# Width-grouped k steps in the two-segment stages, and modulation units summed on all partitions, in a two-layer hybrid trunk

## The reference, cut to what matters

```python
mod_x = jnp.einsum('bd,lde->lbe', jax.nn.silu(c), w_ada) + b_ada[:, None, :]
mod_c = jnp.einsum('d,lde->le', jax.nn.silu(c_ctx), w_ada) + b_ada
for i in range(DEPTH):
    sh1, sc1, g1, sh2, sc2, g2 = jnp.split(mod_x[i][:, None, :], 6, axis=-1)   # and csh1 ... cg2
    hx = rmsnorm(x, norm_mix[i]) * (1.0 + sc1) + sh1                           # hc likewise
    ox, oc = gla_mixer(...) if i % N_MIXERS == 0 else swa_mixer(...)
    x = x + g1 * ox
    x = x + g2 * swiglu(rmsnorm(x, norm_ffn[i]) * (1.0 + sc2) + sh2, ffn_w_in[i], ffn_w_out[i])
    # ctx likewise, except in the last layer
return rmsnorm(x, norm_final)
```

## Time and profile before

| | |
|---|---|
| median of 3 runs (lowest, highest) | 1669.13 us (1669.12, 1671.03) |
| profiled execution, own time | 1669.12 us |
| its span | 1667.4 us |
| mean granted clock of TensorE | 0.989 of 2.4 GHz |
| TensorE matmul busy | 1618.1 us, 9568 matmuls |
| VectorE busy | 864.4 us |
| ScalarE busy | 577.4 us |
| DMA | 156.07 MB, mean 94 GB/s |

### The profile page before, as it was taken

One profiled execution on the slowest core, in us unless ns is written; L12 is line 12 of the kernel. 1 busy time (PEld: TensorE's weight loads), 2 busy tenths in 40 slices (PEclk: granted clock), 3 DMA queues, 4 the chain that ended last, 5 costly groups with the idle time before them and its releaser, 6 DMA issues.

```text
span 1667.4 us, 24130 instructions
## 1 busy us (share of the span) xinstructions
PE 1618.1 (97%) x9568; PEld 1370.2 (82%) x9568; DVE 864.4 (52%) x1426; ACT 577.4 (35%) x833; POOL 99.2 (6%) x96
## 2 busy tenths in 40 slices
PE   7999999999999999999999999979999999999998
PEld 5889988888888888888888888757778788888886
DVE  5314436644576566556566336678755533333334
ACT  4315447542432111122102124457744422222223
POOL 0000000000000000000000000036540000000003
PEclk8999999999999999999999999979999999999999
DMA  9341310013443433343343213320003232333332
GB/s 335 100 128 54 106 44 26 26 51 102 127 127 101 125 127 112 115 126 102 125 126 103 74 57 108 101 76 2 1 1 101 76 101 87 90 100 101 101 88 88
DMA packets 197310, 156.07 MB, mean 94 GB/s; under 512 B 6691, under 2 KB 194255, under 8 KB 197231
## 3 DMA queue, kind: packets, MB, share of 16 engines
q1 hardware_dynamic: 197230, 154.97, 30.4%
HBM read 149.71 MB, written 2.10 MB: 91 GB/s over the span
## 4 chain that ended last, share of the span: by engine, by line
PE 88%; DVE 4%; ACT 4%; issue 1%; SPq 1%; DMA 1%; DVEq 0%; ACTq 0%
PE ps L577 85%; PE ps L1110 1%; ACT w_hi L1189 1%; DVE w_lo L1667 1%; DMA ada_pre<-in_w_ada 1%; PE ps L1115 1%; SPq L376 1%; DVE q_st L2192 1%; DVE h_lo L1730 1%; DVE scaled L1721 0%; ACT h_hi L1239 0%; ACT pr L1624 0%; DMA q_sw<-q_rot 0%; PE ps L892 0%; SPq L495 0%
## 5 line engine op out<-in xcount | busy, mean ns | idle before, releaser
L577 PE MATMUL ps<-h_hi,w_hi 128*128 128x256 f32 (+1 forms) x1392 | 422.3, 362 | 6.9 <-DVE w_lo L1667 6.8
L577 PE MATMUL ps<-h_hi,w_lo 128*128 128x256 f32 (+1 forms) x1392 | 413.6, 355 | 0.0
L577 PE MATMUL ps<-h_lo,w_hi 128*128 128x256 f32 (+1 forms) x1392 | 410.1, 353 | 0.0
L1667 DVE TENSOR_TENSOR w_lo<-w_raw,w_hi 128x2048 fp32r<-128x2048 f32 (+1 forms) x88 | 197.2, 2240 | 219.1 <-ACT w_hi L1189 218.9
L577 PEld LDWEIGHTS ps<-h_hi,w_hi 128*128 128x128 f32 x1392 | 257.3, 190 | 51.9 <-issue 13.5
L1189 ACT ACTIVATE w_hi<-w_raw 128x2048 fp32r<-128x2048 f32 (+1 forms) x88 | 165.1, 1876 | 386.0 <-DMA w_raw<-in_ffn_w_in 207.3
L577 PEld LDWEIGHTS ps<-h_lo,w_hi 128*128 128x128 f32 x1392 | 263.7, 189 | 38.3
L577 PEld LDWEIGHTS ps<-h_hi,w_lo 128*128 128x128 f32 x1392 | 262.9, 189 | 37.0
L577 PE MATMUL ps<-a_hi,w_hi 128*128 128x512 f32 (+1 forms) x528 | 160.5, 359 | 0.0
L577 PE MATMUL ps<-a_hi,w_lo 128*128 128x512 f32 (+1 forms) x528 | 160.1, 358 | 0.0
L577 PE MATMUL ps<-a_lo,w_hi 128*128 128x512 f32 (+1 forms) x528 | 158.0, 354 | 0.0
(11 more groups left out here) (246 smaller groups left out, 2011.7 us busy)
## 6 DMA issues: line engine op xcount, KB each, us to landing
w_raw<-in_ffn_w_in SPq DMA_DIRECT2D x88, 512.0 KB, 4.9
ada_w<-in_w_ada SPq DMA_DIRECT2D x41, 1024.0 KB, 5.3
w_raw<-in_ffn_w_out SPq DMA_DIRECT2D x32, 512.0 KB, 4.4
w_raw<-in_gla_w_in SPq DMA_DIRECT2D x24, 512.0 KB, 4.9
ada_pre<-in_w_ada SPq DMA_DIRECT2D x7, 1024.0 KB, 11.8
w_raw<-in_ffn_w_out SPq DMA_DIRECT2D x16, 384.0 KB, 3.5
w_raw<-in_gla_w_o SPq DMA_DIRECT2D x8, 512.0 KB, 7.2
w_raw<-in_swa_w_o SPq DMA_DIRECT2D x8, 512.0 KB, 5.0
```

Source lines behind the costliest of these rows:

```text
L577: return pe.matmul(o, w, r, start=start, stop=stop, skip_group_check=skip)
L1667: dve.tensor_tensor(w_lo[s][:, 0:kc, :], raw_of(n)[:, 0:kc, :], w_hi[s][:, 0:kc, :].bitcast(F32), ALU.subtract).then_inc(wlo_ok, 1)
```

## The change

**Order in a k step.** Wherever both segments are worked, the segment becomes the outer loop, latent first. So a k step runs its six 512-column matmuls and then its six of 256 (three and three in `fill` and the gate columns).

**Units.** Units 0 to 3 and 12 and 13 leave TensorE, so that 34 of 40 are accumulated by `unit_acc`. The units of FFN 0 move two slabs back, 12 to 39 in slabs 18 to 45. The sum over partitions becomes a product with an fp32r block of ones, 128 x 128, which leaves the sum on all partitions: ScalarE writes the high part of `u_acc` (`unit_high`), VectorE the low part (`unit_low`), and TensorE runs two matmuls of 512 columns into bank 7. VectorE's `store_sum` then multiplies the bank by the identity in blocks of 128, reduces each block to one number a partition, and adds the bias. In the q/k stage the sums stand ahead of k = 1 and 7 of slab 2, k = 6 of slab 3, and the third tile of V0; VectorE accumulates each unit ahead of a split or after it. `ones_r` is copied once for each of two placements of the buffers. The loops of part 0 of an FFN in SyncE's queue become four single rounds.

```diff
@@ slab (and likewise step, first_slab, fill, the gate columns)
-                    for ch in chunks:
-                        blk = slice(ch * P, (ch + 1) * P)
-                        for j, (w, r) in enumerate(((w_hi, x_hi), (w_hi, x_lo), (w_lo, x_hi))):
-                            for sg in segs:
+                    for sg in reversed(segs):
+                        for ch in chunks:
+                            blk = slice(ch * P, (ch + 1) * P)
+                            for j, (w, r) in enumerate(((w_hi, x_hi), (w_hi, x_lo), (w_lo, x_hi))):
@@ unit_sum
             pe.wait_ge(mod_ok, a + 1 + i)
-            pe.wait_ge(ada_done, a + 1 + i)
-            for e in range(2):
-                for m in range(2):
-                    last = mm(bank(6, 2 * e + m, 1), u_acc[:, m, e * P:(e + 1) * P], ones[:, 0:1], True, True)
+            pe.wait_ge(ul_ok, sum_no(a) + 1 + i)
+            for j, u in enumerate((u_hi, u_lo)):
+                last = mm(bank(7), ones_r[u_set(a)][:, :], u[u_set(a)][:, :, :].rearrange("p m n -> p (m n)"), j == 0, j == 1)
             last.then_inc(turned, 1)
@@ first_slab: full unit of the last k steps
-                    if turn is not None:
-                        unit(turn + 1)
@@ TensorE, q/k slabs 2 and 3, gate columns
-        unit(0)
-        slab(QK0 + 2, 0, h_in, BOTH, turns=0, before={5: lambda: unit(1), 7: lambda: unit_turn(1)})
-        unit(2)
-        slab(QK0 + 3, 0, h_in, BOTH, turns=2)
-        unit(3)
+        pe.wait_ge(or_ok, 1)
+        slab(QK0 + 2, 0, h_in, BOTH, before={1: lambda: unit_sum(0), 7: lambda: unit_sum(1)})
+        slab(QK0 + 3, 0, h_in, BOTH, before={6: lambda: unit_sum(2)})
         pe.wait_ge(gwl_ok, 1)
-        pe.wait_ge(row_ok, V0)
+        pe.wait_ge(mod_ok, V0)
@@ TensorE, ffn
-                         before={1: lambda: unit_turn(a), 4: lambda: unit(a + 1), 7: lambda: unit_turn(a + 1)}
-                         if has_unit(n) else {})
@@ ScalarE
+        def unit_high(a, i=0):
+            act.wait_ge(ada_done, a + 1 + i)
+            act.wait_ge(turned, a + 1 + i)
+            if a == 0:
+                act.wait_ge(wlo_ok, QK0 + 3)
+            act.activation(u_hi[u_set(a)][:, :, :], u_acc[u_set(a)][:, :, :], ACT.Copy).then_inc(row_ok, 1)
@@ ScalarE, up (and after the split in the w_out slabs)
                 if ahead:
                     split(n + 1, i, kc)
+                if a_ is not None:
+                    unit_high(a_, i * 2)
@@ VectorE
+        def unit_low(a, i=0):
+            dve.wait_ge(row_ok, a + 1 + i)
+            dve.tensor_tensor(u_lo[u_set(a)][:, :, :], u_acc[u_set(a)][:, :, :], u_hi[u_set(a)][:, :, :].bitcast(F32),
+                              ALU.subtract).then_inc(ul_ok, 1)
+
+        def store_sum(a, i=0):
+            dve.wait_ge(turned, a + 2 + i)
+            part = u_acc[u_set(a)][:, :, :].rearrange("p m (e n) -> p (m e) n", n=P)
+            dve.tensor_tensor(part, bank(7).rearrange("p (c n) -> p c n", n=P),
+                              ident[:, :].rearrange("p (o n) -> p o n", o=1).to_broadcast([P, 4, P]), ALU.mult)\
+               .then_inc(up_ok, 1)
+            dve.wait_ge(up_ok, 2 * sum_no(a) + 1 + i * 2)
+            dve.tensor_reduce(den[:, :], part, AX.X, ALU.add).then_inc(up_ok, 1)
+            dve.wait_ge(up_ok, 2 * sum_no(a) + 2 + i * 2)
+            e = unit_cols(a) + i * 2
+            dve.tensor_tensor(mods[:, bass.ds(e, 2), :], den[:, :].rearrange("p (m e) -> p e m", m=2),
+                              v3(vec[:, bass.ds(V_BADA + e, 2)], 2), ALU.add).then_inc(mod_ok, 1)
@@ VectorE, q/k stage
+        dve.tensor_copy(ones_r[0][:, :], ones[:, :]).then_inc(or_ok, 1)
+        unit_acc(0)
         split(QK0 + 2)
-        store_unit(0)
+        unit_low(0)
+        store_sum(0)
+        unit_acc(1)
         split(QK0 + 3)
-        store_unit(1)
-        store_unit(2)
+        unit_low(1)
+        store_sum(1)
+        unit_acc(2)
         split(QK0 + 4)
+        unit_low(2)
@@ behind g_wlo
-        store_unit(3)
+        store_sum(2)
+        unit_acc(3)
+        unit_low(3)
+        store_sum(3)
@@ VectorE, up (and the w_out slabs)
                 if ahead:
                     split(n + 1, i, kc)
                 if a_ is not None:
-                    store_unit(a_, i * 2)
+                    unit_low(a_, i * 2)
+                    store_sum(a_, i * 2)
@@ SyncE
+        load_unit(1)
         load_slab(3, 0, cols(gla_w_in[0], 768))
-        load_unit(1)
```

More of the change, by code:

```diff
@@ L465, in ffn @@
                 j0 = 0
-                for pairs in ((2, 2), (4,), (2, 1))[PARTS.index((f0, fc))]:
+                for pairs in ((1, 1, 1, 1), (4,), (2, 1))[PARTS.index((f0, fc))]:
                     m = n + 2 * j0
@@ L695, in step @@
             pe.wait_ge(h_ok, 2 * k + 2)
[L696 to L699, removed]
+            for sg in (LAT, CTX):
+                for ch in range(2):
+                    blk = slice(ch * P, (ch + 1) * P)
+                    for j, (w, x_) in enumerate(((w_hi, h_hi), (w_hi, h_lo), (w_lo, h_hi))):
                         last = mm(seg(b0, ch, sg), w[s][:, k, blk], x_[:, k, sg[0]:sg[1]], start=(k == 0 and j == 0 and
@@ L796, in first_slab @@
                     last.then_inc(bw_done, 1)
-                    if turn is not None:
-                        unit(turn + 1)
                 pe.wait_ge(rl_ok, 8 * e + k + 1)
[L800 to L803, removed]
+                for sg in reversed(segs):
+                    for ch in range(2):
+                        blk = slice(ch * P, (ch + 1) * P)
+                        for j, (w, r) in enumerate(((w_hi, raw_hi), (w_hi, raw_lo), (w_lo, raw_hi))):
                             last = mm(seg(b0, ch, sg), w[s][:, k, blk], r(e, k, sg), start=(k == 0 and j == 0 and
@@ L877, in fill @@
                     pe.wait_ge(out_free[s], n // 2)
[L878 to L879 removed]
+            for sg in reversed(BOTH):
+                for j, (w, x) in enumerate(((w_hi, h_hi), (w_hi, h_lo), (w_lo, h_hi))):
                     last = mm(seg(b0, ch, sg), w[s][:, k, blk], x[:, k, sg[0]:sg[1]], start=(k == 0 and j == 0 and
@@ L1015, in ffn @@
                 if lead:
-                    first_slab(n, 2 * l, segs, turn=unit_of(n) - 1 if has_unit(n) else None)
-                    a = unit_of(F0)
-                    slab(n + 1, 0, h_in, segs, k_wait=h_wait(2 * l + 1, per),
-                         before={1: lambda: unit_turn(a), 4: lambda: unit(a + 1), 7: lambda: unit_turn(a + 1)}
-                         if has_unit(n) else {})
+                    first_slab(n, 2 * l, segs, turn=U1 - 1 if l == 0 else None)
+                    slab(n + 1, 0, h_in, segs, k_wait=h_wait(2 * l + 1, per))
+                    if l == 0:
+                        pe.wait_ge(or_ok, 2)
                 m = n + 2 * lead
@@ L1024, in ffn @@
                     for e in range(2):
-                        slab(m + e, i, h_in, segs, sums=unit_of(m) + e if has_unit(n) else None)
+                        slab(m + e, i, h_in, segs, sums=unit_of(m) + e if has_unit(m) else None)
                 if after:
                     for e in range(2):
-                        slab(n + fc - 2 + e, 0, h_in, segs)
+                        m = n + fc - 2 + e
+                        slab(m, 0, h_in, segs, sums=unit_of(m) if has_unit(m) else None)
                 n += fc
@@ L1312, in _ @@
         split(QK0 + 4)
+        unit_high(2)
         qk_out(QK0 + 3)
-        unit_row(3)
+        unit_high(3)
         act.wait_ge(gl_done, 1)
@@ L1502, in ffn @@
                             split(n + e + 1, i)
+                            if has_unit(n):
+                                unit_high(unit_of(n) + e, i * 2)
                 else:
@@ L2033, in plain @@
                 store_unit(unit_of(n))
+        dve.wait_ge(go_ok, 2 * GH)
+        dve.tensor_copy(ones_r[1][:, :], ones[:, :]).then_inc(or_ok, 1)
         scale_rows(32, V_NFFN)
```

72 lines of the change are left out of this document (38 added, 34 removed).

## The result

| | before | after |
|---|---|---|
| median of the runs taken side by side (lowest, highest, runs) | 1670.08 us (1669.12, 1673.90, 4) | 1650.90 us (1650.28, 1653.04, 4) |
| ratio of the times, 95% interval | | 0.9883 (0.9864 to 0.9902) |
| profiled execution, own time; span | 1669.12; 1667.4 us | 1651.26; 1649.5 us |
| mean granted clock of TensorE | 0.989 | 0.987 of 2.4 GHz |

What follows compares the result with a forecast made beforehand. TensorE, busy 97% of the span, was taken as the bound. Gains of 5.9 + 1.5 + 18.9 + 0.1 = 26.4 us off 1669.1 gave 1642.7 us; own range 1640 to 1647, whole range 1640 to 1652.

Steps and rivals of the forecast that it cites:

- rival 1: In FFN 0 the wide spacing survives the grouping, or the sums bring it in: 1651.5 us, chance 0.12.
- Units' sums: FFN 0 from slab 19 to 49: old sums 22.3 us go, new ones 12.2 come, gain 10.1 us.
- VectorE keeps up: FFN 0 slabs: VectorE finishes a unit's low part before its sum at k = 7, margin 1.3 us.
- Rivals 2 and 3: VectorE late at k = 7 in FFN 0: rival 2, 1650 to 1660, chance 0.10; rival 3, 1671, chance 0.02.
- Entry of FFN 0: Slabs 16 and 17: TensorE sheds 3.3 us, 1.4 gained, the rest becomes a wait for w_lo.
- the price of a change of width in a grouped k step: Two-segment k steps: one change to each width costs 3.3 ns a k step, half of a 6.6 ns upper bound.
- the prediction's own sign: In the new trace, a grouped 512 or 256 spacing other than 227 and 120 ns would show the prediction wrong.
- Where the pairs run narrow now, grouping is worth nothing: Narrow two-segment k steps, mostly ahead of FFN 0's loops: grouped 2.080 us equals today's 2.080, gain 0.
- The clock, allowed at 1.5 us either way: Attention and layer 1: no edit, gain 0, but work moves 26 us earlier against 1.2 GHz stretches; 1.5 us either way.

Runs made afterwards that it cites:

- run 1: The changed kernel with the old order in every two-segment k step (256 and 512 columns in turn), new units kept: 1654.74 us, ratio 0.9895.
- run 8: The changed kernel with four more VectorE operations of 512 columns ahead of each unit_low in FFN 0: 1681.43 us, ratio 1.0054.
- run 4: run 1 with four small fp32 matmuls of one column, once, ahead of slab 18: 1654.97 us, ratio 0.9898.
- run 12: The kernel before with only the order within a pair changed, the latent's matmul first: 1663.87 us, ratio 0.9964.

## Why the prediction was right, and what it missed

The gain and its largest term came as reckoned, but the centre was 8 us too low and the forecast's own range, 1640 to 1647, was missed. The time is inside the whole range by 1.1 us only. It landed beside rival 1's 1651.5 by a sum of other misses, which is luck: 4.3 us in the loops of FFN 0, 0.4 at the entry, 0.4 and 0.5 for the order up to V0 and in w_o, 0.7 and 1.5 for the clock in the same two, and 0.7 behind KV0.

- **Units' sums, the largest term (10.1 us): right.** A new sum is 0.47 us, and run 1 shows the whole term.
- **VectorE keeps up: right.** Durations as in their like rows, no wait at a sum, 1.5 us of room (forecast 1.3). Rivals 2 and 3 are refuted by the waits, and run 8 shows where they would have begun.
- **Entry of FFN 0: right.** TensorE stands still for 473.17 - 471.81 - 0.12 = 1.24 us ahead of slab 18, released by w_lo (forecast about 1.4). The stretch gained 1.0 instead of 1.4, since its 16 k steps ran at 2.100 to 2.120 us.
- **The step that failed: the price of a change of width in a grouped k step.** "I take half, 3.3 ns", with 6.6 as the upper bound. The trace has 20 ns: 28 more in the 512s, 8 less in the 256s. The bound was wrong as a bound. It took the wide pairs as the dearest that changes can be, but a spacing averaged over twelve matmuls with a change at each one didn't say what a lone change costs behind five equal matmuls. In pairs, six changes each way cost 0 (2.080) or 40 ns (2.120) a k step, while one each way costs 20. This missed 4.1 us in FFN 0. By the prediction's own sign ("a grouped 512 or 256 spacing other than 227 and 120", they are 231 and 119 in the mean) this part was wrong.
- **"Where the pairs run narrow now, grouping is worth nothing": wrong by the same price.** There it costs 20 to 40 ns a k step: 0.4 us from slab 2 to V0 and 0.5 in w_o. Ahead of slab 2, nine k steps ran at 2.120 us in the change and 2.080 in before, but slab 2's start differs by up to 2.6 us between kernels of one code, so no loss can be read there.
- **Rival 1, the wide spacing survives the grouping, half true.** It gave 1651.5, and the kernel takes 1650.9, but by another sum: grouping did remove half of the wide spacing's cost. What stands is its remark on pairs, that nothing in the code explains them: up to slab 2, before and run 1 have the same loop and run at 2.080 and 2.120 us.
- **The clock, allowed at 1.5 us either way, was put in the wrong place.** The allowance was for attention and layer 1, where the change takes 0.2 us less than before up to the output. The stretches at 1.2 GHz that cost something came in w_o (1.5 us) and ahead of slab 2 (0.7). The 0.7 behind KV0 is the writing of the output.

By the isolated spacing in the Trainium skill ("TensorE: Matmul & The Clock Gate", section Back-to-back issue gap) a k step would take, as an estimate, 6 x 325 ns = 1.95 us, and that formula has no term for the order. These runs show 2.080, 2.090, 2.100 and 2.120 at full granted clock, for the same twelve matmuls in different orders, so here it gives neither the size nor the order's effect.

Shown by runs: the parts of the gain, the price of a change and its scaling with their number, VectorE's room, and that the order within a pair decides the spacing in the loops. The prices of the clock stretches, 1.5 us in w_o and 0.7 ahead of slab 2, rest on one pair of traces each. Open: why a change of width costs anything, why a pair pattern is narrow or wide, what starts either outside the loops, and why the clock fell in w_o in every trace but those of before and run 4. The order of a pair together with whole-slab order elsewhere wasn't tried.

## What to carry to other kernels

Read the cost of mixing matmul widths from the very pattern that the kernel will run. Neither streams of one width nor an alternating pattern bounded what one change costs here. Long streams (a whole slab of each width) or alternating pairs that begin with the wider one were both worth 4.5 us more in FFN 0 than groups of six, and the second is one word in a loop. But pairs that begin with the wider one ran wide in w_o, so the trace of each stage has to be read. Moving a sum over partitions to two wide matmuls plus three more VectorE operations pays where VectorE has room ahead of the sum. That room can be measured by adding operations: 1.4 us more a slab cost one wait, 2.86 cost one in each of 20 slabs. And a trace is one execution: cut it into stretches and compare those with the same code first, before a difference of 1 or 2 us in the total is put down to an edit.

## What the hardware did that I had not expected

- The same twelve matmuls take 2.080 or 2.120 us with the widths alternating. In before, narrow, the starts are 230 and 117 ns apart in turn (347). Wide, they repeat every three pairs:

```
wide:    235 114 232 118 241 120   = 1060 for three pairs
narrow:  230 117 230 116 230 117   = 1040
```

  Either holds for hundreds of pairs, and from slab 18 to KV0 it turned only at a unit sum. No run here shows why.
- In a grouped k step the distance behind the first two 256-column matmuls is 7 and 1 ns short of a stream's 120, and that behind the six of 512 columns is 0.3 to 8 ns over a stream's 226.7.
- Stretches of 3.4 us at 1.2 GHz come and go between executions of near-identical code: one begins between 357 and 365 us in the change and in every run but 4 (in run 12 it lasts 6.8 us), and before has none. It costs 1.5 us, as much as 75 k steps' worth of order; one at 48 us costs 0.7.
